# Block kernel: conditioning slices by chunk pairs and another order of the beginning

## The chip, the cores and the metric

The kernel runs on one NeuronCore of a Trainium2 chip. The metric is the device time of one execution in microseconds (us); lower is better. A profiled execution gives a trace of every instruction on the engines: TensorE (PE, with its weight loads PEld), VectorE (DVE), ScalarE (ACT), GpSimd (POOL) and SyncE (SP, which only issues transfers here). Times of the trace count from the start of the span.

## What is computed

A backbone of four layers over 256 latent tokens and 256 context tokens with 1024 features. Each sub-layer normalizes its input and modulates it with a shift and a scale that come from the conditioning:

```python
def rms_norm(x, gain):
    y = x32 * lax.rsqrt(jnp.mean(x32 * x32, axis=-1, keepdims=True) + EPS)
    return (y * gain.astype(F32)).astype(x.dtype)

def modulate_norm(x, gain, shift, scale):
    return rms_norm(x, gain) * (1 + scale) + shift

# layer i: six vectors of 1024 for each stream (mx: latents, mc: context)
mx = split(silu(c) @ ada_w[i] + ada_b[i], 6)   # shift, scale, gate, twice; mc likewise from c_ctx
hx = modulate_norm(xs, norm_mix[i], mx[0], mx[1])
# layer 0: q, k, v = split(h @ na_w_qkv); q and k normalized by head; attention; @ na_w_o
```

Layers 0 and 3 mix tokens by neighbourhood attention, layer 1 by retention, layer 2 by a convolution; each is followed by a gated feed-forward part. The change lies wholly ahead of and inside the first four weight tiles of layer 0.

## The kernel before

All data lie feature-major: X is 128 partitions x 8 chunks (C = 8) x 512 tokens (context first, then latents). A matrix product in 32-bit precision is made of three products of reduced form: the weights are split into Whi (by ACT) and Wlo (by DVE, L1568), the input into Hhi and Hlo, and `three` (L672 to L674) multiplies high by high, high by low and low by high. A tile is 128 output features: 8 chunks, 24 products, into one PSUM bank. Weights come in groups of 512 KB into the four slots of `raw`.

The beginning of the program, ahead of layer 0:

- SP issues the three FIRST_CONSTS (bias_ada, one, ident), then slices 0 and 2 of the conditioning weights (ada_raw, four quarters of 512 KB each), four weight groups, then slices 1 and 3. A slice is 512 columns of ada_w: slices 0 and 1 are the shifts of chunks 0 to 3 and 4 to 7, slices 2 and 3 the scales of the same chunks. ACT issues the conditioning input c, then X in one transfer of 2 MB, then the eight CONSTS.
- PE spreads the conditioning vectors over the partitions (L1157), which needs FIRST_CONSTS; ACT copies that to `cond`. `first_slice` (L771 through `ada_product`) multiplies a slice in eight products; four of them run side by side in strips of the array. `idle_products` (L668) are transposes whose result nobody reads. `ada_cols` (L785) transposes the rows that DVE has copied from PSUM into hb (L1680); DVE then sums the strips (L1620) and adds the bias (L1622).
- ACT squares X chunk by chunk. DVE adds chunks 0 to 3 and POOL chunks 4 to 7, and `first_norm_sum` (L805) sums over features with 8 products of two columns. ACT takes the root, DVE inverts it and makes a diagonal (L1632), and `norm_spread` (L852) spreads it over the partitions.
- `first_scale` (L1687) makes the scales of four chunks. `first_chunks`: for each chunk DVE multiplies X by scale and norm for each stream (L1706), ACT adds the shift and makes Hhi (L1545), DVE makes Hlo (L1698). Chunks 0 to 3 come first; DVE makes the splits of the first four groups ahead of and between them; then slices 1 and 3 are stored and chunks 4 to 7 follow.

PE's order in `first_tiles`: chunks 0 and 1 of tiles 0 and 1, slice 1 (the third in order), chunks 2 and 3; transposes; tile 2 chunks 0 to 3; slice 3; tile 3 chunks 0 and 1; transposes; tile 3 chunks 2 and 3; then chunks 4 to 7 of tiles 0 and 1, and of tile 2. Then head_sum(0) (L884, the squares of a head of q or k summed), slice 4, the rest of tile 3, head_sum(1), head_sum(2). Every engine works through its own list in order and waits on semaphores; nothing is planned at run time. The instructions of POOL behind this (the bias tables, L575 and L580) wait for four finished slices; DVE needs the tables ahead of the products for V.

Of the kernel before, what the change touches and what calls it, by code (L numbers as in the profile page):

```python
# [30 lines left out]
P = 128  # L31
D = 1024
# [41 lines left out]
FIRST_SLICES = (0, 2, 1, 3)  # L74
FIRST_BANKS = (5, 6, 6, 4)
# [119 lines left out]
def build(nc, x, ada, weights, ada_in, ada_bias, gain, na_gain, rpb, na_mask, rope, decay, dist, gn_gain,  # L195
# [3 lines left out]
    with ctx:  # L199
# [114 lines left out]
        x_loaded = sem("x_loaded")  # L314
# [16 lines left out]
        first_added = sem("first_added")  # L331
        first_added_too = sem("first_added_too")
# [140 lines left out]
        FIRST_CONSTS = [(ada_bias, bias_ada), (ones, one), (identity, ident)]  # L473
# [9 lines left out]
        def _(sp):  # L483
            for src, dst in FIRST_CONSTS:
                full = dst[tuple(slice(None) for _ in dst.shape)]
                sp.dma_start(full, src).then_inc(first_loaded, 16)
            for nth, piece in enumerate(FIRST_SLICES):
                if nth == 2:
                    for s in range(SLOTS):
                        sp.dma_start(raw[:, s, :], weights[s, :, :]).then_inc(raw_loaded[s], 16)  # L490
                for q in range(4 * piece, 4 * piece + 4):
                    sp.dma_start(ada_raw[:, q, :], ada[q, :, :]).then_inc(first_ada[q], 16)

# [34 lines left out]
        def _(pool):  # L528
# [70 lines left out]
            for c in range(5, C):  # L599
                pool.wait_ge(first_squared, c + 1)  # L600
                if c > 5:
                    pool.wait_ge(first_added_too, c - 5)
                g.tensor_tensor(first_squares[:, c, :], first_squares[:, c - 1, :], first_squares[:, c, :], ALU.add)\
                    .then_inc(first_added_too, 1)
# [57 lines left out]
        def _(pe):  # L662
# [138 lines left out]
            def first_norm_sum():  # L801
                for n, (done, c) in enumerate(((first_added, 3), (first_added_too, 7))):
                    pe.wait_ge(done, 3)
                    for b in range(TB):
                        last = t.matmul(bank[4][:, 2 * b:2 * b + 2], first_squares[:, c, P * b:P * b + P], one[:, 0:2],  # L805
                                        start=n == 0 and b == 0, stop=n == 1 and b == TB - 1)
                last.then_inc(norm_summed, 2)

            def first_slice(nth, idle=0):
                if nth >= 2:  # L810
                    pe.wait_ge(rows_copied, nth)
                for k in range(C):
                    q = 4 * FIRST_SLICES[nth] + k // 2
                    if k % 2 == 0:
                        idle_products(idle, 3)
                        pe.wait_ge(first_ada[q], 16)
                    last = ada_product(bank[FIRST_BANKS[nth]], k, ada_raw[:, q, 512 * (k % 2):512 * (k % 2) + 512])
                last.then_inc(ada_rows_made, 1)
# [58 lines left out]
            def na(layer, p):  # L877
# [9 lines left out]
                for nth, tok in ((0, ALL), (1, XT if last_layer else ALL)):  # L887
                    for i, first in ((0, True), (1, False)) if layer == 0 else peeled(pe, 2):
# [292 lines left out]
        def _(act):  # L1181
# [338 lines left out]
            act.dma_start(cfull[:, :, :], ada_in).then_inc(c_loaded, 16)  # L1520
            act.wait_ge(c_loaded, 16)
# [3 lines left out]
            act.dma_start(X[:, :, :], x).then_inc(x_loaded, 16)  # L1525
            for src, dst in CONSTS:
                full = dst[tuple(slice(None) for _ in dst.shape)]
                act.dma_start(full, src).then_inc(const_loaded, 16)
            a.preload_act_table(ACT.Sqrt)
            for r in range(2):  # L1530
# [4 lines left out]
            act.wait_ge(x_loaded, 16)  # L1535
            for c in range(C):
                a.activation(first_squares[:, c, :], X[:, c, :], ACT.Square).then_inc(first_squared, 1)
            act.sem_inc(last_squared, 2)
# [3 lines left out]
            for c in range(C):  # L1542
# [4 lines left out]
                if c < 2:  # L1547
                    split(Step(c + 2 - LEAD))
# [14 lines left out]
        def _(dve):  # L1563
# [51 lines left out]
            def ada_store(index, piece=None):  # L1615

                piece = index if piece is None else piece
# [4 lines left out]
                v.tensor_tensor(mod_slices[:, bass.ts(piece, 4), :], ada_sum[:, :, :],  # L1622
# [650 lines left out]
```

## Time and profile before

| | us |
|---|---|
| median of 3 runs | 2507.7 |
| lowest, highest | 2506.86, 2510.31 |
| span of the profiled execution | 2503.2 |
| PE busy in it | 2433.3 (97%) |
| DVE busy | 1816.1 (73%) |
| ACT busy | 1065.2 (43%) |
| POOL busy | 652.6 (26%) |

The device time holds the span and some microseconds around it. The page gives sums over the whole execution, and the change concerns its first 75 us, so the timeline of the single engines there says more.
### The profile page before, as it was taken

The numbers are of one execution on the slowest core, as the hardware profiler recorded it, in microseconds if no ns is written. First come the engines' busy times: TensorE is split into PE (matmuls) and PEld (weight loads), VectorE is DVE, ScalarE is ACT, GpSimd is POOL, SyncE is SP. The second block draws the span as 40 slices with busy tenths as digits, with TensorE's granted clock in tenths as the row PEclk, the third lists the DMA queues.
The fourth block names the chain that finished last, engine by engine and source line by source line (L and its number), as shares of the span: only waits on it lengthen the run. The fifth ranks groups of instructions, "written<-read, shape, count | busy, mean of one in ns | idle before, by whom it ended". The sixth has DMA issues, their size and how long they took to land. (4 is left out here: it accounts for less than half of the span.)

```text
span 2503.2 us, 36222 instructions
## 1 busy us (share of the span) xinstructions
PE 2433.3 (97%) x12655; PEld 2003.5 (80%) x12655; DVE 1816.1 (73%) x2653; ACT 1065.2 (43%) x1679; POOL 652.6 (26%) x442
## 2 busy tenths in 40 slices
PE   7998899999999999999999999999999999998999
PEld 4675588888888868888888888778888888867999
DVE  4886569888974355427888768987988876855874
ACT  3335534443231244414444227863544324455543
POOL 2414233332300020022333224844333324101000
PEclk9999999999999999999999999999999999999999
DMA  7642025555633321224545542213555554312555
GB/s 270 178 167 76 10 84 171 173 172 192 220 103 101 103 74 51 96 98 135 174 169 173 181 142 77 67 33 111 169 175 168 185 176 125 120 51 68 186 183 186
DMA packets 94890, 337.48 MB, mean 135 GB/s; under 512 B 11840, under 2 KB 13632, under 8 KB 94656
## 3 DMA queue, kind: packets, MB, share of 16 engines
q1 hardware_dynamic: 67136, 240.38, 28.7%
q10 hardware_dynamic: 24768, 86.74, 10.5%
q0 software_dynamic: 2880, 8.92, 1.7%
q8 instruction: 70, 1.15, 0.2%
q14 instruction: 36, 0.29, 0.0%
HBM read 334.95 MB, written 1.05 MB: 134 GB/s over the span
## 5 line engine op out<-in xcount | busy, mean ns | idle before, releaser
L672 PE MATMUL bank<-Hhi,Whi 128*128 128x512 f32 (+1 forms) x2416 | 866.2, 359 | 25.2 <-DVE Wlo L1568 8.4
L674 PE MATMUL bank<-Hhi,Wlo 128*128 128x512 f32 (+1 forms) x2416 | 853.5, 353 | 0.0
L673 PE MATMUL bank<-Hlo,Whi 128*128 128x512 f32 (+1 forms) x2416 | 853.1, 353 | 0.0
L1568 DVE TENSOR_TENSOR Wlo<-raw,Whi 128x1024 fp32r<-128x1024 f32 x424 | 636.4, 1502 | 225.0 <-ACT Whi L1186 207.2
L1186 ACT ACTIVATE Whi<-raw 128x1024 fp32r<-128x1024 f32 x424 | 448.1, 1059 | 749.2 <-DMA raw<-in_weights 695.4
L672 PEld LDWEIGHTS bank<-Hhi,Whi 128*128 128x128 f32 x2416 | 457.1, 189 | 104.1 <-issue 30.5
L673 PEld LDWEIGHTS bank<-Hlo,Whi 128*128 128x128 f32 x2416 | 457.4, 189 | 63.8 <-issue 2.6
L674 PEld LDWEIGHTS bank<-Hhi,Wlo 128*128 128x128 f32 x2416 | 457.4, 189 | 63.0
L545 POOL TENSOR_TENSOR cond_w<-cond_w,cond 128x1024 f32<-128x1024 f32 x107 | 259.3, 2423 | 599.8 <-DVE square L1592 514.7
L672 PE MATMUL bank<-Ghi,Whi 128*128 128x512 f32 (+1 forms) x770 | 268.5, 349 | 0.0
L674 PE MATMUL bank<-Ghi,Wlo 128*128 128x512 f32 (+1 forms) x770 | 266.7, 346 | 0.0
L673 PE MATMUL bank<-Glo,Whi 128*128 128x512 f32 (+1 forms) x770 | 264.9, 344 | 0.0
L537 POOL TENSOR_TENSOR square<-X 128x512 f32<-128x512 f32 (+1 forms) x51 | 80.5, 1578 | 449.9 <-DVE X L1748 441.4
L674 PEld LDWEIGHTS bank<-Ghi,Wlo 128*128 128x128 f32 x770 | 144.5, 188 | 20.3
L673 PEld LDWEIGHTS bank<-Glo,Whi 128*128 128x128 f32 x770 | 144.5, 188 | 19.6
L672 PEld LDWEIGHTS bank<-Ghi,Whi 128*128 128x128 f32 x770 | 144.7, 188 | 17.5
L1592 DVE SCALAR_TENSOR_TENSOR hb<-cond_w,cond 128x1024 f32<-128x1024 f32 x113 | 155.4, 1376 | 3.8
L1506 ACT ACTIVATE hb<-hb 128x512 f32<-128x512 f32 (+1 forms) x88 | 51.0, 580 | 210.5 <-DVE hb L2111 210.5
L1592 DVE SCALAR_TENSOR_TENSOR square<-cond_w,cond 128x1024 f32<-128x1024 f32 x99 | 121.2, 1225 | 11.7
L1203 ACT ACTIVATE cond_w<-cond_w 128x1024 f32<-128x1024 f32 x107 | 112.5, 1051 | 37.6 <-POOL cond_w L545 36.3
L643 POOL TENSOR_TENSOR pooled<-pooled,products 128x512 f32<-128x512 f32 x68 | 105.1, 1545 | 33.1 <-ACT products L1469 24.5
L1803 DVE RECIPROCAL na_root<-na_root 128x512 f32<-128x512 f32 (+1 forms) x32 | 94.3, 2947 | 19.1 <-ACT na_root L1266 19.1
(267 smaller groups left out, 2990.8 us busy)
## 6 DMA issues: line engine op xcount, KB each, us to landing
raw<-in_weights SPq DMA_DIRECT2D x424, 512.0 KB, 3.4
cond_w<-in_ada ACTq DMA_DIRECT2D x160, 512.0 KB, 3.8
ada_raw<-in_ada SPq DMA_DIRECT2D x16, 512.0 KB, 16.0
ada_ring<-in_ada SPq DMA_DIRECT2D x16, 512.0 KB, 7.4
rel_in<-in_rpb POOLq DMA_DIRECT2D x48, 128.0 KB, 4.8
decay_t<-in_dist POOLq DMA_DIRECT2D x4, 640.0 KB, 4.3
X<-in_x ACTq DMA_DIRECT2D x1, 2048.0 KB, 10.7
out_y<-X SPq DMA_DIRECT2D x1, 1024.0 KB, 4.8
```

What stands on the lines that cost most here:

```text
L537: g.tensor_tensor(square[:, c % 2, tok], X[:, c, tok], X[:, c, tok], ALU.mult).then_inc(sum_step, 1)
L545: g.tensor_tensor(w, w, cond[:, 0, :], ALU.mult).then_inc(cond_scaled, 1)
L643: g.tensor_tensor(pooled[:, c % 2, :], pooled[:, c % 2, :], products[:, i % PRODUCTS, :], ALU.add).then_inc(pool_added, 1)
L672: t.matmul(dst, Whi[:, st.slot, w], hi, start=start, stop=False)
L673: t.matmul(dst, Whi[:, st.slot, w], lo, start=False, stop=False)
L674: return t.matmul(dst, Wlo[:, st.slot, w], hi, start=False, stop=stop)
L1186: a.activation(Whi[:, st.slot, :], raw[:, st.slot, :], ACT.Copy).then_inc(hi_split, 1)
L1203: a.activation(w, w, ACT.Copy, accum_out=cond_sum[:, n % COND_SLOTS, 0:1]).then_inc(cond_summed, 1)
L1506: a.activation(cv[:, k, tok], cv[:, k, tok], ACT.Gelu_apprx_tanh).then_inc(gelu_done, 1)
L1568: v.tensor_tensor(Wlo[:, st.slot, :], raw[:, st.slot, :], Whi[:, st.slot, :].bitcast(F32), ALU.subtract)\
L1592: last = v.scalar_tensor_tensor(scratch, w, 1.0, cond[:, r, :], ALU.mult, ALU.mult, accum_out=cond_sum[:, slot, r:r + 1])
L1803: v.reciprocal(na_root[:, m, tok], na_root[:, m, tok]).then_inc(qk_rstd, 1)
```

## The change

- The columns of the first four slices are reordered on the host (`_first_pairs`): slice n now holds the shifts and the scales of chunks 2n and 2n+1. `first_store` stores both and makes the scales of the pair.
- X comes first on SP's queue, in four transfers of two chunks; then slice 0, groups 0 and 1, slice 1, group 2, slice 2, group 3, slice 3. FIRST_CONSTS go to ACT's queue, CONSTS to POOL's.
- ACT squares X ahead of copying `cond`. DVE and POOL add no squares; `first_norm_sum` takes all eight chunks in 32 products.
- PE sums the norm right after the spread of the conditioning, then makes slice 0 with idle products ahead of each quarter, the norm spread ahead of its last quarter. Only one slice stands ahead of the first tiles.
- `first_tiles` goes by pairs of chunks: products of a pair, the next slice, its transposes at once, the next pair. DVE's and ACT's weight splits move along.

The diff without the semaphores' declarations and the removed bodies:

```diff
@@ sync
+            for q in range(4):
+                sp.dma_start(X[:, 2 * q:2 * q + 2, :], x[:, 2 * q:2 * q + 2, :]).then_inc(x_loaded[q], 16)
+            first_piece(0)
+            first_group(0)
+            first_group(1)
+            first_piece(1)
+            first_group(2)
+            first_piece(2)
+            first_group(3)
+            first_piece(3)
@@ gpsimd
-            for c in range(5, C):
...
-                g.tensor_tensor(first_squares[:, c, :], first_squares[:, c - 1, :], first_squares[:, c, :], ALU.add)\
-                    .then_inc(first_added_too, 1)
+            for src, dst in CONSTS:
+                full = dst[tuple(slice(None) for _ in dst.shape)]
+                g.dma_start(full, src).then_inc(const_loaded, 16)
@@ tensor
             def first_norm_sum():
-                for n, (done, c) in enumerate(((first_added, 3), (first_added_too, 7))):
-                    pe.wait_ge(done, 3)
+                for c in range(C):
+                    pe.wait_ge(first_squared, c + 1)
...
+            def first_slice(nth, quarters, idle=0):
+                if nth:
                     pe.wait_ge(rows_copied, nth)
+                for q in quarters:
+                    idle_products(idle, 3)
+                    pe.wait_ge(first_ada[4 * nth + q], 16)
+                    for k in (2 * q, 2 * q + 1):
+                        last = ada_product(bank[6], k, ada_raw[:, 4 * nth + q, 512 * (k % 2):512 * (k % 2) + 512])
+                    if q == 3:
+                        last.then_inc(ada_rows_made, 1)
...
                 pe.wait_ge(tile_free, p["mix_tile"] + 4)
-                for k in range(4):
+                for k in (0, 1):
                     for m in range(2):
                         first_tile(steps[m], m, (k,))
-                    if k == 1:
-                        first_slice(2)
-                ada_cols(2)
-                first_tile(steps[2], 2, range(4))
-                first_slice(3)
-                first_tile(steps[3], 3, (0, 1))
-                ada_cols(3)
-                first_tile(steps[3], 3, (2, 3))
-                for k in range(4, C):
+                first_slice(1, range(4), 5)
+                ada_cols(1)
+                for k in (2, 3):
                     for m in range(2):
                         first_tile(steps[m], m, (k,))
-                first_tile(steps[2], 2, range(4, C))
+                first_tile(steps[2], 2, range(4))
+                first_slice(2, range(4))
+                ada_cols(2)
+                for k in (4, 5):
+                    for m in range(2):
+                        first_tile(steps[m], m, (k,))
+                first_tile(steps[2], 2, (4, 5))
+                first_tile(steps[3], 3, range(6))
+                first_slice(3, range(4))
+                ada_cols(3)
+                for k in (6, 7):
+                    for m in range(2):
+                        first_tile(steps[m], m, (k,))
+                first_tile(steps[2], 2, (6, 7))
...
                             head_sum(0, 0, tok)
+                            first_tile(steps[3], 3, range(6, C))
+                            head_sum(1, 1, tok)
                             ada_slice(0)
-                            first_tile(steps[3], 3, range(4, C))
-                            head_sum(1, 1, tok)
                             head_sum(2, 2, tok)
...
-            first_slice(0)
+            first_norm_sum()
+            pe.wait_ge(cond_ready, 2)
+            first_slice(0, range(3), 5)
+            norm_spread(0, ALL)
+            first_slice(0, (3,), 5)
             ada_cols(0)
-            pe.wait_ge(cond_ready, 2)
-            first_slice(1, 5)
-            first_norm_sum()
-            ada_cols(1)
-            idle_products(14, 3)
-            norm_spread(0, ALL)
-            idle_products(8, 3)
+            idle_products(12, 3)
@@ scalar
+            for src, dst in FIRST_CONSTS:
+                full = dst[tuple(slice(None) for _ in dst.shape)]
+                act.dma_start(full, src).then_inc(first_loaded, 16)
...
+            for c in range(C):
+                if c % 2 == 0:
+                    act.wait_ge(x_loaded[c // 2], 16)
+                a.activation(first_squares[:, c, :], X[:, c, :], ACT.Square).then_inc(first_squared, 1)
...
-                if c < 2:
-                    split(Step(c + 2 - LEAD))
+                if c in (3, 5):
+                    split(Step(c // 2 + 1 - LEAD))
@@ vector
+            for nth in range(FIRST_SLICES):
+                if nth:
+                    dve.wait_ge(h_ready, 4 * nth)
+                first_store(nth)
+                if nth == 0:
+                    dve.wait_ge(norm_rstd, upto(0, ALL))
+                    first_chunk(0, [Step(-LEAD)])
+                    split(Step(1 - LEAD))
+                    first_chunk(1)
+                else:
+                    first_chunk(2 * nth)
+                    first_chunk(2 * nth + 1)
+                if nth in (1, 2):
+                    split(Step(nth + 1 - LEAD))
```

`first_store` now holds the copy of the rows (L1680 of before), the wait for the transposes, the sum of the strips, the bias and the scales of the pair; `first_chunk(c, between)` holds for one chunk the two products, the splits of `between`, and the two low parts.

## Rows read from the trace of the kernel before

**Rows 1.** The profile's page: its first line, and TensorE in part 1.

```profile
span 2503.2 us, 36222 instructions
...
PE 2433.3 (97%) x12655; PEld 2003.5 (80%) x12655; DVE 1816.1 (73%) x2653; ACT 1065.2 (43%) x1679; POOL 652.6 (26%) x442
```

**Rows 2.** Timeline of PE, beginning: start, length (us), line, operation, count, [idle before].

```profile
5.12 6.35 PE L1157 MATMUL bank<-ident,csilu 128*128 128x128 f32 x32 [5.12 <-DMA ident<-in_identity]
...
19.11 1.05 PE L771 MATMUL bank<-ada_raw,csilu 128*32 128x512 f32 x4
20.09 0.77 PE L668 MATMUL bank<-ident 128*128 128x128 f32 x5
...
25.12 1.95 PE L805 MATMUL bank<-one,first_squares 128*128 128x2 f32 x16
26.93 0.64 PE L785 MATMUL bank<-ident,hb 128*128 128x128 f32 x4
...
29.15 1.10 PE L852 MATMUL bank<-root,one 128*128 128x512 f32 x2
...
33.54 0.47 PE L672 MATMUL bank<-Hhi,Whi 128*128 128x512 f32 x1 [2.42 <-DVE Hlo L1698]
```

**Rows 3.** Timeline of DVE, same columns.

```profile
25.24 0.69 DVE L1680 COPY hb<-bank 128x512 f32<-128x512 f32 x1 [5.34 <-PE bank L771]
...
29.19 2.36 DVE L1568 TENSOR_TENSOR Wlo<-raw,Whi 128x1024 fp32r<-128x1024 f32 x2
...
52.55 0.19 DVE L1620 TENSOR_REDUCE ada_sum<-bank 128x8 f32<-128x32 f32 x1 [1.32 <-PE bank L785]
...
53.25 0.87 DVE L1706 SCALAR_TENSOR_TENSOR hb<-X,scale,bank 128x256 f32<-128x256 f32 x2
54.30 0.88 DVE L1698 SCALAR_TENSOR_TENSOR Hlo<-hb,mod,Hhi 128x256 fp32r<-128x256 f32 x2 [0.18 <-ACT Hhi L1545]
```

**Rows 4.** Timeline of PE through the first tiles.

```profile
38.50 0.63 PE L672 MATMUL bank<-Hhi,Whi 128*128 128x512 f32 x1
...
39.91 2.52 PE L771 MATMUL bank<-ada_raw,csilu 128*32 128x512 f32 x16
...
43.17 0.40 PE L672 MATMUL bank<-Hhi,Whi 128*128 128x512 f32 x1
43.40 0.39 PE L673 MATMUL bank<-Hlo,Whi 128*128 128x512 f32 x1
...
48.54 1.92 PE L771 MATMUL bank<-ada_raw,csilu 128*32 128x512 f32 x16
...
55.33 0.47 PE L672 MATMUL bank<-Hhi,Whi 128*128 128x512 f32 x1 [1.43 <-DVE Hlo L1698]
...
65.07 1.02 PE L884 MATMUL bank<-na_sq,one_head 128*128 128x512 f32 x2
...
74.54 0.79 PE L672 MATMUL bank<-Hhi,Whi 128*128 128x512 f32 x1
```

**Rows 5.** ACT's queue (start, length of issue); transfers 0 to 30 us, KB, us to landing.

```profile
3.43 0.45 ACTq L1528 DMA_DIRECT2D gains<-in_gain  x1
...
7.21 2.02 ACTq L1528 DMA_DIRECT2D one_head<-in_head_ones  x1
...
one_head<-in_head_ones ACTq DMA_DIRECT2D x1, 64.0 KB, 18.3
gains<-in_gain ACTq DMA_DIRECT2D x1, 32.0 KB, 11.7
```

**Rows 6.** Windows of PE: us, busy, PEclk, DMA share, GB/s; with one timeline row.

```profile
34.30:36.00 1.70, 1.46 (x4) 0.51 1.01 402
42.00:44.00 2.00, 2.00 (x12) 1.00 0.02 6
...
1565.91 0.47 PE L672 MATMUL bank<-Hhi,Whi 128*128 128x512 f32 x1 [2.70 <-DVE Wlo L1568]
...
1567.00:1568.00 1.00, 1.00 (x4) 0.50 0.00 0
```

More of the change, by code:

```diff
@@ L73 @@
 ADA_START = 4
-FIRST_SLICES = (0, 2, 1, 3)
-FIRST_BANKS = (5, 6, 6, 4)
+FIRST_SLICES = 4
 ADA_QK = 4
@@ L313, in build @@
         const_loaded = sem("const_loaded")
-        x_loaded = sem("x_loaded")
+        x_loaded = [sem(f"x_loaded{q}") for q in range(4)]
         hi_split = sem("hi_split")
@@ L471, in halves @@
             return ((1, XT),) if tok == XT else ((0, CT), (1, XT))
-        FIRST_CONSTS = [(ada_bias, bias_ada), (ones, one), (identity, ident)]
+        FIRST_CONSTS = [(identity, ident), (ones, one), (ada_bias, bias_ada)]
         CONSTS = [(gain, gains), (na_gain, qk_gain), (na_mask, mask),
@@ L1524, in _ @@
             a.activation(csilu[:, :, 0:2], cfull[:, :, :], ACT.Silu).then_inc(c_ready, 1)
[L1525 to L1528, printed above, removed]
             a.preload_act_table(ACT.Sqrt)
+            for c in range(C):
+                if c % 2 == 0:
+                    act.wait_ge(x_loaded[c // 2], 16)
+                a.activation(first_squares[:, c, :], X[:, c, :], ACT.Square).then_inc(first_squared, 1)
+            act.sem_inc(last_squared, 2)
             for r in range(2):
@@ L1534, in _ @@
                 last.then_inc(cond_ready, 1)
[L1535 to L1538, printed above, removed]
             root_of_norm(0, ALL)
@@ L1678, in first_store @@
             def first_store(nth):
+                pair = slice(2 * nth, 2 * nth + 2)
                 dve.wait_ge(ada_rows_made, nth + 1)
-                v.tensor_copy(rows[:, :], bank[FIRST_BANKS[nth]][:, :]).then_inc(rows_copied, 1)
-                ada_store(nth, FIRST_SLICES[nth])
-            def first_scale(half, done):
-                at = slice(4 * half, 4 * half + 4)
-                dve.wait_ge(mod_ready, 8 * (half + 1))
-                v.scalar_tensor_tensor(scale[:, 0, at, :], mod[:, 0, C + 4 * half:C + 4 * half + 4, :], 1.0,
-                                       gains[:, 0, 0, at].unsqueeze(2).to_broadcast([P, 4, 2]),
-                                       ALU.add, ALU.mult).then_inc(done, 1)
-                dve.wait_ge(done, 1)
@@ L1692, in first_chunks @@
-            def first_chunks(first, end, splits):
-                def low(n):
-                    c, half = divmod(n, 2)
-                    hs = XT if half else CT
+                v.tensor_copy(rows[:, :], bank[6][:, :]).then_inc(rows_copied, 1)
+                dve.wait_ge(cols_made, nth + 1)
+                strips = bank[7][:, :].rearrange("p (q j r) -> p q r j", j=4, r=QUAD)[:, :, 0:2, :]
+                v.tensor_reduce(ada_sum[:, :, :], strips, axis=AX, op=ALU.add).then_inc(strips_added, 1)
@@ new lines, in first_store, with first_chunk @@
+                done = scale_ready if nth == FIRST_SLICES - 1 else first_scaled
+                v.scalar_tensor_tensor(scale[:, 0, pair, :], mod[:, 0, C + 2 * nth:C + 2 * nth + 2, :], 1.0,
+                                       gains[:, 0, 0, pair].unsqueeze(2).to_broadcast([P, 2, 2]),
+                                       ALU.add, ALU.mult).then_inc(done, 1)
+                dve.wait_ge(done, 1 if nth == FIRST_SLICES - 1 else nth + 1)
+            def first_chunk(c, between=()):
+                for half, hs in halves(ALL):
+                    n = 2 * c + half
+                    if n >= 4:
+                        dve.wait_ge(h_ready, n - 3)
+                    v.scalar_tensor_tensor(ring[n % 4][:, hs], X[:, c, hs], scale[:, 0, c, half:half + 1],
+                                           spread_bank(0, ALL)[:, hs], ALU.mult, ALU.mult).then_inc(norm_scaled, 1)
+                for st in between:
+                    split(st)
+                for half, hs in halves(ALL):
+                    n = 2 * c + half
@@ L1699, in low @@
                                            Hhi[:, c, hs].bitcast(F32), ALU.add, ALU.subtract).then_inc(h_ready, 1)
-                for c in range(first, end):
-                    for half, hs in halves(ALL):
-                        n = 2 * c + half
-                        if n >= 4:
-                            dve.wait_ge(h_ready, n - 3)
-                        v.scalar_tensor_tensor(ring[n % 4][:, hs], X[:, c, hs], scale[:, 0, c, half:half + 1],
-                                               spread_bank(0, ALL)[:, hs], ALU.mult, ALU.mult).then_inc(norm_scaled, 1)
-                        if half:
-                            low(n - 1)
-                    low(2 * c + 1)
-                    if c < len(splits):
-                        split(splits[c])
             def norm_halves(r, tiles, add_half, following):
```

64 lines of the change are left out of this document (18 added, 46 removed).

## The prediction

> **What bounds the kernel now.** I read part 1 of the page first: TensorE (PE) is busy 2433.3 of 2503.2 us [rows 1], so nearly everything that delays PE delays the end, and all idle time of PE together is 69.9 us. The change touches only the beginning, so I then read PE's timeline there [rows 2], next to VectorE's (DVE) [rows 3]. Until 33.5 us PE does no tile product: it spreads the conditioning, makes slices 0 and 2, sums the squares, spreads the norm. From 33.54 on come the first four weight tiles. They end, for the comparison below, where head_sum(0) starts, at 65.07 [rows 4]; twelve products (tile 3, chunks 4 to 7) are still owed there. Behind it a chain through DVE leads to the next tile at 74.54 [rows 4], and from there PE is the bound. The question is thus when head_sum(0) starts in the changed kernel, and what is owed there.
>
> **Up to the first product.** PE's order becomes: spread, norm sums, three quarters of slice 0, norm spread, last quarter, transposes.
> - *Start.* The spread waits for the three first constants, as now (5.12, [rows 2]). They move from SP's queue, where nothing was ahead, to ACT's, behind c, while the four 512 KB parts of X go first on SP. Eight small transfers queued on ACT beside the big ones are the nearest row: gains landed at 3.43+11.7 = 15.1, one_head at 7.21+18.3 = 25.5, so (25.5-15.1)/7 = 1.48 us each [rows 5]. Bounds: 5.1 (contention costs nothing) and 5.1+3x1.48 = 9.5. I take 7.2, a little under the middle, as part of the queueing is already in the 5.1.
> - Beside that number: the Trainium skill, DMA: Bandwidth & Descriptors, section Queues, rings and completion order, says that a DMA engine takes turns between queues and does a whole packet of one before it switches. By that rule a small transfer pays a turn of a large one whatever its bytes, which agrees with a step of 1.48 us on the mean of seven small transfers; by a share of bytes the constants would land near 5.1 and the whole sum would be 2.1 us lower.
> - *Spread of the conditioning*: 6.3 us, unchanged (start 5.12, length 6.35, [rows 2]).
> - *Norm sums.* Now 8 products are 16 records from 25.12 to the next start at 26.93 [rows 2]: 0.113 us a record. All eight chunks without sums beforehand are 32 products, 64 records: 7.2 us. The squares are no limit: X, now first, lands its 2 MB before the spread is over, and ACT is free then. So DVE's and GpSimd's six additions go (they lay beside other work) and PE pays 5.4 us more. Bounds: 7.8 by the row's own length (1.95 for 16); below, if products of two columns overlapped twice as well in a long train, 3.6. I take 7.2, since the 16 records are the same instruction.
> - *Slice 0 with idle products*: a quarter is 20.09-19.11 = 0.98, the five idle products ahead of it (25.12-19.11-4x0.98)/3 = 0.70 [rows 2]. Three quarters: 5.0. Norm spread 0.9 (1.10 by its row, of which the next work covers a little). Last quarter 1.7. DVE's inversion, 1.4 us behind the norm sums, is hidden under the quarters. The pieces of slice 0 have landed: 4 MB by then.
> - Sum: 7.2+6.3+7.2+5.0+0.9+1.7 = 28.3.
> - *Return trip to DVE*: copy of the rows from the end of the slice 25.12 to 25.24+0.69 = 0.81 [rows 2, 3]; transposes 0.64 [rows 2] and 0.05 of wake-ups; sum of the strips to first chunk 53.25-52.55 = 0.70 [rows 3]. 2.2 us. I call the start of chunk 0 S: S = 30.5.
> - Chunk 0 then: two products 0.85, one weight split in between 1.18 (2.36 for two), two low parts 0.88 [rows 3]: first tile product at S+3.0 = 33.5, against 33.54: one slice less ahead of it (6.0 us) is paid back by the norm sums, the later constants and the splits between.
>
> **The first tiles.** Here the order is what costs. All relative to S.
> - Chunk 1: DVE's second split 1.15, products and low parts, so PE has it at S+6.0. PE is at half clock by then: it waits 2.2 us ahead of the first product, and after 2.42 us of waiting the clock was 0.51 [rows 2, 6]; a product then takes 0.43: three in 39.91-38.50 = 1.41, the switch to the slice included [rows 4]. Six take 2.6: S+8.6.
> - Slice 1 stands here with 5 idle products ahead of each quarter: 4x1.68 = 6.7, and about 0.9 for the rest of the slow stretch (slice 1's place now: 2.52 against 1.92, [rows 4]). S+16.2. Its pieces are behind X, slice 0 and two weight groups, some 7.4 MB, which at the beginning's rate are in long before (the sixteen pieces, X and the rest are all through by 42 us now, [rows 6]), so the idle products cover no wait: they cost 6.7-1.92 = 4.8 us.
> - Now transposes (ada_cols) follow each slice at once, with no products between. PE waits for DVE's copy, then for the whole return trip and the first chunk: 2.2 + 1.93 (two products, ACT's high part, two low parts: 53.25 to 54.30+0.88, [rows 3]) + 0.1 = 4.25 us from the end of a slice to the next product, three times (slices 1, 2, 3). At present products lie between, and the one wait of this kind is 1.43 us [rows 4]. 12.8 us, of which the transposes (1.9) are work in either kernel. Queued behind these waits on PE are all products of the earlier chunks that could have filled them.
> - Each such wait leaves PE idle 2.7 us at a stretch. After 2.70 us of waiting at 1565.91 the clock was 0.50 [rows 6]. So each pair begins slow: about eight products at 0.43 instead of 43.40-43.17 = 0.23 [rows 4]. The second chunk of the pair follows 1.9 us behind the first (DVE's rows at 53.25 and 54.30 and the wait between, [rows 3]), which hides some of it: a pair takes 1.9+2.46 = 4.36 instead of 3.3. The Trainium skill, TensorE: Matmul & The Clock Gate, section HAM oscillation, says that bursts between waits pay the slow start at every burst; the two rows agree, and without it the sum would be 2.7 lower.
> - From S+16.2: trip 4.25, pair 2 (k 2, 3) 4.36, tile 2 with 12 products 2.8: S+27.6. Slice 2 1.92, trip 4.25, pair 3 4.36, 24 products 5.5: S+43.6. Slice 3 1.92, trip 4.25, pair 4 4.36, 6 products 1.4: S+55.5, rounded for the splits that are just in time.
> - head_sum(0) at 30.5+55.5 = 86.0, against 65.07: 20.9 later. Only six products are owed behind it instead of twelve, but the way to the next tile goes over DVE (reciprocal and copy of rows) and keeps about 9.5 us; I give 0.5 back for ACT's earlier turn. Sum: +20.4.
>
> **Moved issues.** The eight other constants go to GpSimd's queue, ahead of the bias tables, which start at slice 3's end anyway; they were in at 25.5 on ACT [rows 5]; GpSimd is idle then, and they are first needed at about S-9, 21 us in. Weight groups 0 to 3 move between the pieces; group 3 stands ahead of slice 3's pieces and so is in well before its split at S+37. Bounds 0 to +1; I take 0. GpSimd's bias tables begin 20 us later and then share the transfers with refills: 0 to +1.5, I take 0.
>
> **Rivals.** The expected case is A: clock slow at each pair, +20.4 (18 to 24), chance 0.72.
> - B: the clock stays up between slices. For it: the wait of 1.43 us left it up. Against: the waits of 2.42 and 2.70 us [rows 2, 6]. 20.4-2.7 = +17.7. Chance 0.14.
> - C: the change does better than the sums: constants in at 5.1 (-2.1), norm sums at half price (-3.6), and the slow start absent (-2.7): about +12. Chance 0.07, since each is at its bound.
> - D: transfers in the new order come late: slice 1's pieces, behind X and two weight groups, arrive after PE asks at S+8.6 = 39.1. Decides only if the rate at the start fell by half; +25 or more. Chance 0.03.
> - E, the other side: not slower, because the delay is taken up behind. After 75 us PE idles about 55 of the 69.9 us [rows 1]; if 21 us of that were waits for something that doesn't move with the first tiles (weight transfers, bias tables), the end would stay. It decides from about 21 us of such waits, and then gives 0, at most -6 if the later start also spares contention. Against: PE works on what the first tiles give and DVE's chains follow it. Chance 0.04 (0.02 for each side of the bound).
>
> **How the numbers follow.** The profiled span is 2503.2; the median of the timed runs is 2507.7, some 4.5 around the span, which the change doesn't touch. 2507.7+20.4 = 2528.1. Range: from C's neighbourhood, +10, to the upper bounds (constants 9.5, slow start full) +25: 2518 to 2533. A measurement here tells about 0.2% (5 us). Faster 0.02, same 0.03, slower 0.95.
>
> **What would show it.** Right: records of the norm sums 64 and 7.2 us long; first tile product at 32 to 36; three PE waits of about 2.7 us ending in a low part of a chunk, clock 0.5 after them; slice 1 some 7 us long with no DMA wait; head_sum(0) near 86; the rest shifted as a block. Wrong: head_sum(0) before 75; DMA waits ahead of slices; a stretch behind 100 us that has become shorter.

## Result: 1.2% slower

| | before | changed |
|---|---|---|
| median | 2507.28 us (4 runs) | 2538.12 us (4 runs) |
| lowest, highest | 2505.38, 2510.31 | 2533.50, 2540.49 |
| span of the profiled execution | 2503.2 | 2538.0 |

The ratio is 1.012 with a 95% interval of 1.0106 to 1.0134. The forecast was slower by 20.4 us within a range up to 2533; measured are 30.8, outside the range. The first line of the page and its row of PE, the answer to [rows 1]:

```profile
span 2538.0 us, 36336 instructions
...
PE 2453.4 (97%) x12713; PEld 2020.2 (80%) x12713; DVE 1811.3 (71%) x2652; ACT 1065.6 (42%) x1679; POOL 651.6 (26%) x447
```

PE has 58 more records and 20 us more of busy time, and the span is 34.8 us longer. So more than half of the loss shows up as work of PE, not as idle time. The timeline of PE, which answers to [rows 2] and [rows 4]:

```profile
10.92 6.21 PE L1168 MATMUL bank<-ident,csilu 128*128 128x128 f32 x32 [10.92 <-DMA bias_ada<-in_ada_bias]
16.96 11.46 PE L809 MATMUL bank<-one,first_squares 128*128 128x2 f32 x64
28.29 1.31 PE L672 MATMUL bank<-ident 128*128 128x128 f32 x5
29.53 1.92 PE L775 MATMUL bank<-ada_raw,csilu 128*32 128x512 f32 x4
...
43.25 0.76 PE L676 MATMUL bank<-Hhi,Whi 128*128 128x512 f32 x1 [2.37 <-DVE Hlo L1719]
...
46.24 0.67 PE L676 MATMUL bank<-Hhi,Whi 128*128 128x512 f32 x1
...
53.57 1.05 PE L775 MATMUL bank<-ada_raw,csilu 128*32 128x512 f32 x4
55.49 0.66 PE L789 MATMUL bank<-ident,hb 128*128 128x128 f32 x4 [0.86 <-DVE hb L1690]
58.96 0.47 PE L676 MATMUL bank<-Hhi,Whi 128*128 128x512 f32 x1 [2.82 <-DVE Hlo L1719]
...
72.74 0.47 PE L676 MATMUL bank<-Hhi,Whi 128*128 128x512 f32 x1 [2.81 <-DVE Hlo L1719]
...
89.44 0.77 PE L676 MATMUL bank<-Hhi,Whi 128*128 128x512 f32 x1 [3.06 <-DVE Hlo L1719]
...
95.98 1.02 PE L895 MATMUL bank<-na_sq,one_head 128*128 128x512 f32 x2
...
105.75 1.42 PE L676 MATMUL bank<-Hhi,Whi 128*128 128x512 f32 x1
```

Read against the old rows: the start at 10.92 instead of 5.12; 64 records of norm sums that take 11.33 us (16.96 to 28.29) where 16 took 1.81; the idle products and the first wave of slice 0 behind them at nearly twice their old length (1.31 and 1.92 against 0.77 and 1.05); the first tile product at 43.25 instead of 33.54; then a wait of 2.8 to 3.1 us ahead of each pair, at 58.96, 72.74 and 89.44. The first head sum starts at 95.98 instead of 65.07, the next tile at 105.75 instead of 74.54: 31.2 us later. From there the rest takes 2432.3 us, against 2428.7 before. In nine of the ten kernels below that remainder is between 2428.1 and 2433.3, whatever stands ahead of it (in e5, 2438.2), so I read the 3.6 us as the spread of single executions, not as the change.

The row of DVE's timeline that is S, the start of chunk 0:

```profile
40.31 0.87 DVE L1712 SCALAR_TENSOR_TENSOR hb<-X,scale,bank 128x256 f32<-128x256 f32 x2
```

S is 40.31. From S to the first head sum are 95.98-40.31 = 55.67 us; the forecast had 55.5, although its parts did not all come out (see the account below). Nearly all of the net error lies ahead of S: 40.3 instead of 30.5. Two views name it. First, windows over the norm sums (us, then busy time and count of PE, PEld, DVE, ACT and POOL, then PEclk, DMA share, GB/s):

```profile
15.00:20.00 5.00, 5.00 (x41) 5.00 (x40) 0.00 (x0) 1.88 (x4) 0.00 (x0) 0.94 1.03 410
20.00:25.00 5.00, 5.00 (x25) 5.00 (x25) 0.00 (x0) 0.00 (x0) 0.00 (x0) 0.50 1.02 408
25.00:30.00 5.00, 5.00 (x24) 4.38 (x25) 0.96 (x3) 1.47 (x3) 0.00 (x0) 0.50 1.03 409
30.00:35.00 5.00, 5.00 (x22) 1.79 (x18) 0.01 (x1) 0.69 (x1) 0.00 (x0) 0.70 1.03 410
```

PE is busy for all 5.00 us of each window and the granted clock is 0.50 all the same. Second, the transfers of the beginning (KB, us from issue to landing); c, ident, one and bias_ada were issued at 0.76, 1.20, 1.69 and 2.18:

```profile
bias_ada<-in_ada_bias ACTq DMA_DIRECT2D x1, 96.0 KB, 8.6
ident<-in_identity ACTq DMA_DIRECT2D x1, 64.0 KB, 5.3
one<-in_ones ACTq DMA_DIRECT2D x1, 64.0 KB, 6.8
...
hb<-in_ada_in ACTq DMA_DIRECT2D x1, 8.0 KB, 4.2
...
gains<-in_gain POOLq DMA_DIRECT2D x1, 32.0 KB, 5.4
...
one_head<-in_head_ones POOLq DMA_DIRECT2D x1, 64.0 KB, 6.4
```

They landed at 5.0, 6.5, 8.5 and 10.8, about 1.9 us apart. GpSimd's eight small constants were issued from 1.31 (gains, the first) to 5.22 (one_head, the last), so they landed from 6.7 to 11.6, only 0.7 us apart.

### The profile page after: what moved, and what is told of

It is laid out like the page before. It is cut to its first block and busy times, and to the rows that moved or that the text cites. A ratio compares the mean times of both kernels' runs of the same rounds, so it can differ in the third digit from the quotient of the medians.

```text
span 2538.0 us, 36336 instructions
## 1 busy us (share of the span) xinstructions
PE 2453.4 (97%) x12713; PEld 2020.2 (80%) x12713; DVE 1811.3 (71%) x2652; ACT 1065.6 (42%) x1679; POOL 651.6 (26%) x447
## 3 DMA queue, kind: packets, MB, share of 16 engines
HBM read 334.95 MB, written 1.05 MB: 132 GB/s over the span
## 5 line engine op out<-in xcount | busy, mean ns | idle before, releaser
L676 PE MATMUL bank<-Hhi,Whi 128*128 128x512 f32 (+1 forms) x2416 | 869.7, 360 | 32.7 <-DVE Hlo L1719 11.1
```

Source lines behind the costliest of these rows:

```text
L676: t.matmul(dst, Whi[:, st.slot, w], hi, start=start, stop=False)
```

## The experiments

All times below are of the profiled execution unless a ratio is given; S and the other landmarks are as above.

| kernel | PE starts | norm sums | S | first head sum | next tile | ratio to before (95%) |
|---|---|---|---|---|---|---|
| before | 5.1 | 1.8 | 31.5 | 65.1 | 74.5 | 1 |
| changed | 10.9 | 11.3 | 40.3 | 96.0 | 105.8 | 1.012 (1.0106 to 1.0134) |
| e1_sums_off_pe | 11.1 | 1.7 | 29.1 | 83.2 | 93.1 | 1.0077 (1.0060 to 1.0094) |
| e2_consts_first | 4.7 | 8.5 | 30.6 | 85.7 | 94.7 | 1.0108 (1.0088 to 1.0129) |
| e3_trips_hidden | 11.1 | 8.9 | 36.6 | 79.1 | 88.5 | 1.0053 (1.0037 to 1.0070) |
| e4_products_between | 11.2 | 10.7 | 40.2 | 95.6 | 104.3 | one run, 2535.9 us |
| e5_before_with_pe_sums | 4.2 | 11.3 | 42.1 | 75.4 | 84.9 | one run, 2524.9 us |
| e6_no_idle_in_slice_1 | 11.0 | 9.2 | 37.9 | 90.7 | 100.5 | one run, 2532.5 us |
| e7_pool_consts_late | 10.1 | 9.1 | 37.0 | 93.4 | 102.2 | one run, 2535.6 us |
| e8_all_together | 5.0 | 1.8 | 22.9 | 58.6 | 67.2 | 0.9979 (0.9970 to 0.9988) |
| e9_wide_norm_sums | 11.3 | 7.1 | 34.1 | 89.1 | 99.0 | 1.0094 (1.0075 to 1.0112) |
| e10_slices_behind_transposes | 5.0 | 1.8 | 23.6 | 56.5 | 65.1 | 0.9967 (0.9955 to 0.9980) |

A train is here a run of such records without a gap. The six kernels whose 64 two-column records stand in a row show how long the train takes from one execution to the next: 8.5, 8.9, 9.1 and 9.2 us (e2, e3, e7, e6) and twice 11.3 (the changed kernel and e5). What differs is when the clock falls: by the means of windows of 1 us it was at 1.00 until 4.8 to 5.5 us into the train in the four short ones, and until 2.4 and 2.6 us in the two long ones. The changed kernel's profiled execution is at the long end.

**The norm sums taken off PE (e1_sums_off_pe).** DVE and GpSimd add again, as before:

```diff
-                for c in range(C):
-                    pe.wait_ge(first_squared, c + 1)
+                for n, (done, c) in enumerate(((first_added, 3), (first_added_too, 7))):
+                    pe.wait_ge(done, 3)
```

> The changed kernel with one part undone: DVE and GpSimd add the squares of four chunks each again, PE sums the norm in 8 products (16 records) instead of 32 (64 records). Theory (the train of two-column products is what lets the clock fall): the norm sums take 1.8 us instead of 11.3, the granted clock stays 1.00 from 15 to 35 us, the quarters of slice 0 behind them return to 1.68 us each, so the first chunk on DVE starts at 40.3-9.5-2.1 = 28.7 us and the kernel is about 11.6 us faster than the changed one (some 2526). Rival (the clock falls there for another reason, as it would behind any long start, and only the number of records counts): the sums save 64 to 16 records at half clock, 8.5 us, the quarters stay slow, first chunk at 31 to 32, about 2529.

PE's row of the sums, and one window behind them (PE's columns alone):

```profile
17.54 1.84 PE L817 MATMUL bank<-one,first_squares 128*128 128x2 f32 x16
```

```profile
20.00:25.00 5.00, 5.00 (x24) 1.00 1.03 411
```

S is 29.1 (28.7 expected), the median 2525.35 us, so the part costs 12.8 us of the 30.8. The clock is 1.00 in every window from 5 to 45 us. This says that the part is to blame, not yet why it costs more than twice the 5.4 us that its 48 additional records were to take.

**The same part alone in the kernel before (e5_before_with_pe_sums).** The sums' additions on DVE and GpSimd go as well.

```diff
-                for n, (done, c) in enumerate(((first_added, 3), (first_added_too, 7))):
-                    pe.wait_ge(done, 3)
+                for c in range(C):
+                    pe.wait_ge(first_squared, c + 1)
```

> The kernel before with one part of the change alone: PE sums all eight chunks of squares in 32 products (64 records), at the old place behind slice 2, and DVE and GpSimd add nothing. Theory (a long train of two-column products lets the clock fall wherever it stands, here behind wide products at full clock): the sums take 8.5 to 11.3 us instead of 1.8, the granted clock is 0.50 in their last part, and the first tile product comes 7 to 10 us later than 33.5, at 40 to 43. Rival (the clock only fell because the changed kernel has its sums right behind the start): clock 1.00, sums 7.2 us, first tile product 5.4 us later, at 39.

PE's timeline, and windows with PE's columns alone:

```profile
24.34 1.05 PE L765 MATMUL bank<-ada_raw,csilu 128*32 128x512 f32 x4
25.32 11.48 PE L799 MATMUL bank<-one,first_squares 128*128 128x2 f32 x64
...
44.20 0.47 PE L666 MATMUL bank<-Hhi,Whi 128*128 128x512 f32 x1 [1.25 <-DVE Hlo L1692]
```

```profile
20.00:25.00 5.00, 5.00 (x29) 1.00 1.04 398
25.00:30.00 5.00, 5.00 (x35) 0.79 1.02 406
30.00:35.00 5.00, 5.00 (x25) 0.50 1.03 410
```

The clock falls within the train here too, although slice 2 with its idle products ran at full clock ahead of it. The sums take 11.34 us and the first tile product comes at 44.20, 10.7 later than before, a little beyond the expected 43. The place behind the start is not the cause. Its one execution took 2524.9 us, some 18 above the kernel before; 10.4 of it is there at the next tile (84.92 against 74.54); the remainder behind it is 2438.2 us, some 5 above every other kernel here, and why was not followed up.

**Wider products between (e4_products_between).** After each chunk's four sums stand four idle transposes of 128 columns:

```diff
                         last = t.matmul(bank[4][:, 2 * b:2 * b + 2], first_squares[:, c, P * b:P * b + P], ...
+                    idle_products(4)
```

> The changed kernel with four idle 128-column transposes put behind each chunk's four norm sums (32 more products). Theory (products of only two columns don't hold the clock, wider ones do): the clock stays 1.00 through the norm sums, they take 7.2 us for the 64 records plus 32 x 0.14 = 4.5 for the transposes, 11.7 in all, as long as without, and the quarters behind them return to 1.68 us, so the first chunk starts about 2 us earlier, near 38.5. Rival (the clock falls there whatever stands in the train): 64 and 64 records at half clock, some 18 us, first chunk at 46 or later.

Windows of this kernel, PE's columns alone (us, busy, PEclk, DMA share, GB/s):

```profile
20.00:25.00 5.00, 5.00 (x49) 1.00 1.03 410
25.00:30.00 5.00, 5.00 (x29) 0.58 1.02 406
```

The clock held through seven of the eight chunks, until about 25.5 us, 8.6 us after the train's start at 16.91, and then fell: 0.58 in the window of 25 to 30. The sums and transposes took 10.7 us to the start of the last transposes, but slice 0 behind them was slow again and S stayed at 40.2. Neither side had this. In the trains without transposes the clock fell 2.4 to 5.5 us after their start, so the fall came later here, in this one execution, but the wider products between didn't prevent it. Counted in two-column records it came after 56, against some 20 to 50 without transposes (an estimate from these times and 0.113 us a record). The expectation of a gain of 2 us is missed.

**The same products, 128 columns wide (e9_wide_norm_sums).**

```diff
-                        last = t.matmul(bank[4][:, 2 * b:2 * b + 2], first_squares[:, c, P * b:P * b + P], one[:, 0:2],
+                        last = t.matmul(bank[4][:, P * b:P * b + P], first_squares[:, c, P * b:P * b + P], one[:, :],
```

The diff shows the products alone; ACT's root reads the first two columns of each block of 128.

> The changed kernel with one size changed: its 32 norm sums multiply the squares by all 128 columns of ones instead of two (same stationary operands, same number of records, ACT reads two columns of each block for the root). Theory (what lets the clock fall is that a product of two columns keeps the array busy for next to nothing, while its weight load takes 0.12 us): the granted clock stays 1.00 from 15 to 35 us, the 64 records take 7.8 to 9 us in spite of 64 times the columns, the quarters behind take 1.68 us, and DVE's first chunk starts at 35.5 to 37 instead of 40.3. Rival (weight loads of such a density or the mere length of the start let it fall): clock 0.50 within 3 to 9 us of the train's start, as in the changed kernel.

PE's timeline over the train, and windows with PE's columns:

```profile
17.09 7.31 PE L809 MATMUL bank<-one,first_squares 128*128 128x128 f32 x64
24.23 0.71 PE L672 MATMUL bank<-ident 128*128 128x128 f32 x5
```

```profile
20.00:25.00 5.00, 5.00 (x47) 1.00 1.04 414
25.00:30.00 5.00, 5.00 (x24) 1.00 1.01 405
```

64 records again, the same weight loads in the same place, 64 times the columns, and the train takes 7.14 us instead of 11.33 at a granted clock of 1.00. That is even under the expected 7.8 to 9, and it is what the prediction had from [rows 2], 7.2. S is 34.1, under the 35.5 to 37 expected, and the median of two runs is 2529.67 us, 8.5 less than the changed kernel. The train is longer than the 5.5 us within which the clock had fallen in all six with two columns. So neither the number of 64 products nor their place is enough: the clock fell when each of the 64 moved two columns. This rests on one profiled execution with 128. The Trainium skill, TensorE: Matmul & The Clock Gate, section What's actually happening, says that the clock is gated by how busy the array has been. The runs agree that what PE does decides, but the busy time of the profile doesn't show it: it is 5.00 of 5 us at 1.00 here and 5.00 of 5 us at 0.50 in the changed kernel.

**The constants ahead of X (e2_consts_first).**

```diff
-                act.dma_start(full, src).then_inc(first_loaded, 16)
+                sp.dma_start(full, src).then_inc(first_loaded, 16)
```

The line moves from ACT's list to SP's, ahead of the parts of X.

> The changed kernel with only the three first constants back on SP's queue, ahead of X. Theory (their turns behind the parts of X and beside GpSimd's small transfers delay the start): PE starts at 5 to 5.5 us instead of 10.9 and everything behind it moves by 5.5 us, the first chunk at about 34.8, the kernel at about 2532.5. Rival (PE would then wait for X's squares or for the pieces of slice 0, which now arrive in the shadow of the late start): PE starts early, but a wait opens ahead of the norm sums or of a quarter, and less than 3 us is gained.

PE's timeline at the start:

```profile
4.70 5.89 PE L1171 MATMUL bank<-ident,csilu 128*128 128x128 f32 x32 [4.70 <-DMA bias_ada<-in_ada_bias]
10.43 8.67 PE L812 MATMUL bank<-one,first_squares 128*128 128x2 f32 x64
18.96 1.31 PE L675 MATMUL bank<-ident 128*128 128x128 f32 x5
```

PE starts 6.2 us earlier than in the changed kernel and no wait opens ahead of sums or quarters. The median is 2531.35 us, 6.8 less, but its four runs spread from 2526.99 to 2539.51, so this number is uncertain by some us. S moved by 9.7 rather than 5.5: 6.2 of this are the start, 2.8 the shorter train of sums (8.5 against 11.3) in that execution, so of the profile only the start is to be read as this edit's gain.

**GpSimd's constants held back (e7_pool_consts_late).**

```diff
+            pool.wait_ge(first_loaded, 16 * len(FIRST_CONSTS))
             for src, dst in CONSTS:
```

> The changed kernel, but GpSimd issues its eight small constants only once the three first ones have landed. Theory (three queues that take turns make each small transfer slower than two did): the steps between the landings on ACT's queue shrink from about 2.0 us to 1.5 and PE starts at 9.3 to 9.7 instead of 10.9 to 11.2. Rival (the parts of X alone set the step): PE starts at 10.9 to 11.2 as before.

The last of the three constants in the list of transfers (issued at 2.18):

```profile
bias_ada<-in_ada_bias ACTq DMA_DIRECT2D x1, 96.0 KB, 7.8
```

PE starts at 10.08, between both expectations: against the 10.9 to 11.3 of the kernels that differ from it only later, 0.8 to 1.2 us of the delay are GpSimd's queue, in one execution. The landings (4.6, 6.0, 8.2, 10.0) are still 1.8 apart, not 1.48. What the further 0.3 is was not tried; the three constants have 64 to 96 KB each where [rows 5] has mostly less.

**The idle products of slice 1 (e6_no_idle_in_slice_1).**

```diff
-                first_slice(1, range(4), 5)
+                first_slice(1, range(4))
```

> The changed kernel without the twenty idle products in slice 1. Theory (its pieces have long landed, so they cover no wait): slice 1 takes 1.9 to 2.5 us instead of 6.7, the first head sum comes 4.3 to 4.8 us earlier, some 2533.5. Rival (the pieces aren't there at that time, or the clock, which the idle products had brought up, stays low for longer and takes the gain back): a wait for a transfer in the slice, or under 2 us gained.

PE's timeline, chunk 1 and slice 1:

```profile
43.82 0.77 PE L676 MATMUL bank<-Hhi,Whi 128*128 128x512 f32 x1 [0.29 <-DVE Hlo L1719]
...
46.65 2.69 PE L775 MATMUL bank<-ada_raw,csilu 128*32 128x512 f32 x16
```

No transfer is waited for, as the theory says. The slice takes 2.69 us instead of 6.7, so removing the idle products saved 4.0 us in it, a little under the expected 4.3 to 4.8, because it began at half clock (1.92 at full). From S to the end of slice 1 are 46.65+2.69-37.9 = 11.4 us instead of 54.6-40.3 = 14.3, only 2.9 less. The missing 1.1 us stand ahead of the place of the edit: the six products of chunk 1 ran at half clock (2.83 us) where the changed kernel had its clock back at 46.7 (1.66 us). An edit behind these products can't be read as the cause of that. From S to the first head sum it is 52.8 against 55.7.

**Another order of PE's list (e3_trips_hidden).** The same instructions:

```diff
                 # chunk 2 of tiles 0 and 1
+                first_slice(2, range(4))
                 # chunk 3 of tiles 0 and 1
-                first_tile(steps[2], 2, range(4))
-                first_slice(2, range(4))
                 ada_cols(2)
+                first_tile(steps[2], 2, range(4))
                 # chunks 4 and 5, slice 3 and the products of tiles 2 and 3 likewise
```

A comment stands for unchanged products; slice 1 likewise moves between chunks 0 and 1.

> The changed kernel with another order of PE's list in the first tiles alone: each next slice stands between the two chunks of a pair, and the products of tile 2 (and of tile 3 for the last) stand behind the transposes instead of ahead of the slice, so they fill the way over DVE. The same instructions. Theory (the trips are exposed by the order, and the clock falls behind each): from the first chunk to the first head sum 55.7 us shrinks by two trips of 4.25 us, 0.8 of the first and two slow starts of 1.0, to about 44; the kernel at about 2527. Rival (DVE's chunks bound the phase, so that waits only move): the waits for low parts of chunks stay at 2.8 us in another place and less than 3 us is gained.

PE's timeline, the products behind waits and behind transposes:

```profile
39.55 0.47 PE L676 MATMUL bank<-Hhi,Whi 128*128 128x512 f32 x1 [2.37 <-DVE Hlo L1722]
...
52.97 0.77 PE L676 MATMUL bank<-Hhi,Whi 128*128 128x512 f32 x1 [2.82 <-DVE Hlo L1722]
...
60.73 0.60 PE L789 MATMUL bank<-ident,hb 128*128 128x128 f32 x4
61.08 0.48 PE L676 MATMUL bank<-Hhi,Whi 128*128 128x512 f32 x1
...
79.06 1.02 PE L898 MATMUL bank<-na_sq,one_head 128*128 128x512 f32 x2
```

From S to the first head sum are 42.5 us instead of 55.7 (44 expected), the median is 2520.6 us, 17.5 less than the changed kernel and 6 under the expected 2527. The wait ahead of chunk 2 is still there (52.97), but behind the transposes at 60.73, and again at 69.07, products follow at once, and none of the later chunks is waited for. So DVE's chunks don't bound the phase; PE's order exposed them. The median gained more than the 13.2 us within the first tiles; 3.7 us more is S in the profiled execution, 2.4 of it a shorter train of sums.

**All terms undone (e8_all_together) and one step more (e10_slices_behind_transposes).** The first keeps the slices by chunk pairs and X in parts, and takes e1, e2 and e3 together, with slice 0 ahead of the norm sums and slice 1 behind the norm spread:

```diff
+            first_slice(0, range(4))
+            pe.wait_ge(cond_ready, 2)
             first_norm_sum()
-            pe.wait_ge(cond_ready, 2)
-            first_slice(0, range(3), 5)
+            ada_cols(0)
+            idle_products(8, 3)
             norm_spread(0, ALL)
-            first_slice(0, (3,), 5)
-            ada_cols(0)
-            idle_products(12, 3)
+            first_slice(1, range(4))
```

The diff shows PE's beginning alone; DVE also stores slice 0 ahead of inverting the root.

> The changed kernel's data layout (slices by chunk pairs, X in four parts) with the terms that cost it undone: first constants ahead of X on SP, squares added on DVE and GpSimd, slice 0 ahead of the norm sums, slice 1 in the gap ahead of the first tile product and without idle products, and the transposes' trips filled with products of tiles 2 and 3. Theory (only one slice is needed ahead of the first tiles, and the order hid that): PE starts at 5, DVE's first chunk at about 20 us, first head sum at 56 to 58, the tile behind it at 66 to 67 against 74.5 in the kernel before, so about 2499, 0.3% faster than before. Rival (the transfers now bind: slice 0, two groups and slice 1 land one behind the other at 0.5 MB in 1.3 us, up to 22 us, slices 2 and 3 up to 35): PE waits for pieces in slices 1 to 3, and the kernel is within 3 us of the one before.

The median is 2501.25 us (11 runs), 0.21% below the kernel before and 2.3 us above the expected 2499. S is 22.9 where 20 was expected, and the first head sum is at 58.57, just beyond the expected 56 to 58; PE waits 0.83 us and three times 0.2 for the quarters of slice 0, and later for none, so the rival is right for the first slice alone. A wait of 2.82 us stood ahead of chunk 2 at 33.68, with the clock at 0.66 in the window behind it. The second puts slices 2 and 3 where that wait is:

```diff
                 ada_cols(1)
+                first_slice(2, range(4))
                 # chunk 2
-                first_slice(2, range(4))
                 # chunk 3
                 ada_cols(2)
+                first_slice(3, range(4))
```

Here too comments stand for unchanged products.

> The kernel e8_all_together with slices 2 and 3 moved from between the chunks of a pair to right behind the transposes of the slice before, on PE's list alone. Theory (the first trip over DVE still left PE idle for 2.82 us at 33.7 and the clock fell behind it; the slice fills 1.9 of it): the wait shrinks to about 0.9, the clock stays 1.00 from 30 to 45, the first head sum comes 3 to 3.5 us earlier, at 55 to 55.5, the kernel 3 us faster than e8_all_together, about 2498. Rival (slice 2 isn't there yet: X, slices 0 and 1 and three groups are ahead of it, 28 us by 0.5 MB in 1.3 us, against PE's 30.8): PE waits for a piece and less than 1 us is gained.

PE's timeline of the last kernel:

```profile
5.03 6.64 PE L1181 MATMUL bank<-ident,csilu 128*128 128x128 f32 x32 [5.03 <-DMA bias_ada<-in_ada_bias]
13.27 1.05 PE L786 MATMUL bank<-ada_raw,csilu 128*32 128x512 f32 x4 [1.60 <-DMA ada_raw<-in_ada]
...
23.48 2.36 PE L786 MATMUL bank<-ada_raw,csilu 128*32 128x512 f32 x16
...
30.98 0.60 PE L800 MATMUL bank<-ident,hb 128*128 128x128 f32 x4
31.51 1.92 PE L786 MATMUL bank<-ada_raw,csilu 128*32 128x512 f32 x16
34.40 0.47 PE L687 MATMUL bank<-Hhi,Whi 128*128 128x512 f32 x1 [0.96 <-DVE Hlo L1729]
...
56.48 1.02 PE L908 MATMUL bank<-na_sq,one_head 128*128 128x512 f32 x2
```

PE waits 1.60 us for slice 0's first piece. The wait ahead of chunk 2 is 0.96 and slice 2 runs at its 1.92 without a wait for a transfer. The first head sum is at 56.48; against S this is 32.9 instead of 35.7 us, 2.8 of the expected 3 to 3.5. The median is 2498.98 us, ratio 0.9967 (0.9955 to 0.9980): the lowest median here, 8 us below the one before. Against e8_all_together the medians differ by 2.3 us of the expected 3, while the single runs of both overlap.

## Why the prediction was wrong, step by step

- *What bounds, and where to look*: right. The delay of 31.2 us at the tile behind the first four reaches the end; the remainder did not shrink (rival E fell).
- *First tiles, from S*: right about the order and the trips, right in the total (55.67 against 55.5) in part by luck. Trips of 4.25 us were forecast; from the end of slice 1 at 55.49-0.86 = 54.63 to the product at 58.96 are 4.33. There were three waits of 2.8 to 3.1 us, each with a fall of the clock behind it. But from S to the end of slice 1 it took 14.3 us and not 16.2, since the clock was back at 46.7, ahead of chunk 1's second product, and from there to the first head sum 41.4 and not 39.3 (the trip and pair 4, for one, took 4.6 and 5.15 us instead of 4.25 and 4.36). Two errors of 2 us cancelled. That the clock was down at the first tile product came true here, but not in e1, e2, e3 and e9 behind the same wait of 2.37 us. Rival B (clock stays up between slices) fell; its price of 2.7 doesn't fit the text's own pairs either, three times 4.36-3.3 = 3.2. Rival D fell too: no slice waited for a transfer.
- *Behind the first head sum*: the 0.5 us given back for ACT's earlier turn didn't come; the way to the next tile took 9.8 us against 9.5.
- *Idle products cover no wait*: right about the wait. Their price of 4.8 us is 4.0 within the slice by e6.
- *Start of PE*: mis-sized. 10.9 was measured, 7.2 taken, and the upper bound 9.5 was too low: 3.7 us. That the place in the queues costs the time is shown by e2 (start at 4.7). c landed at 5.0, 2 us later than before, and the bound of three steps of 1.48 us holds only if the steps do: they were 1.5, 2.0 and 2.3 us. With GpSimd's queue out of the way (e7) they were still 1.8 on average. That every small transfer costs a turn of that size isn't borne out, as GpSimd's constants landed 0.7 us apart beside the same large ones. What sets the step stays open.
- *Norm sums*: the step that failed. "I take 7.2, since the 16 records are the same instruction": the count was right, and so was the price at full clock, as far as e9 shows it with 7.14 us for 128 columns. But the 16 records of the price lasted 1.8 us, and in none of the six trains had the clock fallen by then; the earliest fall came after 2.4 us. The bounds asked only whether the products are cheaper in a long train, never whether the train changes the clock, although the section on the first tiles charged a fallen clock for an idle PE. 4.1 us in the profiled execution (1.3 to 4.1 over the runs), and 2.1 more for slice 0 behind it, at half clock.
- *Sum*: 3.7+4.1+2.1 = 9.9, the distance of S from its forecast (40.3-30.5 = 9.8). In the profiled execution the forecast of 20.4 is missed by 10.8 us at the next tile (31.2): 9.8 ahead of S, 0.2 in the first tiles and 0.8 behind them. The sides of the measured 30.8 us by runs against the changed kernel: 12.8 for the norm sums (e1), 6.8 for the constants (e2), 17.5 for the order of the first tiles (e3), some 37 in all; each is a difference of medians with an uncertainty of a few us, part of e2's and e3's is the varying train of sums, and set against them is the slice that no longer stands ahead of the first tiles, worth 6.0 us in the prediction.
- *Range*: too narrow on the slow side. The upper bounds of start (9.5) and sums (7.8) were each passed, together.
- *Time around the span*: the 4.5 us set a median against the span of another execution. In each run on record the time is 1.8 to 2.5 us above its own span. The sum, a difference, doesn't depend on it.

## What to carry to other kernels

A work item moved to TensorE must be priced with the clock that it leaves behind, not only with its record length: a train of 64 products of two columns looked like full busy time and still brought half clock for itself and for what followed. If an operand chain goes over another engine and back, put the work that doesn't need it behind the start of the trip, not ahead of it; the same instructions in another order gave 17.5 us here. And small transfers that everything waits for belong in front of large ones: PE started at 4.7 instead of 10.9 us.

## What the runs showed of the hardware

The granted clock went from 1.00 to 0.50 while PE was busy without a gap, in six of six executions with 64 two-column records in a row (trains of 8.5 to 11.3 us). It stayed at 1.00 in the one with 128 columns, whose train took 7.1 us. With four 128-column transposes after every eight of these records it held for 8.6 us and then fell too, so what would suffice stays open. 16 such records in a row (before, e1, e8, e10) never brought it down; they last 1.8 us.

The clock also fell behind waits. Each of the 23 waits of 2.8 to 3.1 us ahead of a tile product, in nine kernels, had windows at 0.50 to 0.68 within 2 us of its end. Of the eight waits of 2.37 us ahead of the first tile product, four were followed by half clock within 2 us (changed, e4, e6, e7) and four were not (e1, e2, e3, e9), in the same place of the same list. So whether a wait of that length was followed by a slow start differed from one profiled execution to the next.
